# Two fused transformer blocks with 32 experts on one core: expert 1's count, the place of two norm products, and the order of work among the attention heads

## What is computed

```python
def first_block(x, ...):      # conditioned by c
    h = rmsnorm(x, norm1_g) * (1.0 + sc1) + sh1
    xr, yr, q, k, v, ga, gb = split(h @ w_in)
    y_a = rg_lru(causal_dwconv(xr)) * gelu(yr)
    y_b = stick_breaking_attention(norm(q), norm(k), v)
    x = x + gt1 * ((sigmoid(ga) * y_a + sigmoid(gb) * y_b) @ w_out)
    h2 = rmsnorm(x, norm2_g) * (1.0 + sc2) + sh2
    g_ff, v_ff = split(causal_dwconv(h2 @ ffn_up))
    return x + gt2 * ((gelu(g_ff) * v_ff) @ ffn_down)

def second_block(x, ...):
    h = rms_norm(x, g_pre_mix) * (1.0 + sc1) + sh1
    y_mla = mla_attention(...)     # 8 heads
    y_dsa = dsa_attention(...)     # 8 heads, keys picked by an index score
    x = x + gt1 * rms_norm(concat(y_mla, y_dsa) @ w_o, g_post_mix)
    h2 = rms_norm(x, g_pre_ffn) * (1.0 + sc2) + sh2
    # each token goes to its 4 best of 32 experts:
    #   hid = x @ w_mlp1[e] + b1; glu/lin halves; act @ w_mlp2[e] + b2
    return x + gt2 * rms_norm(moe_ffn(h2), g_post_ffn)
```

## Time and profile before

| | |
|---|---|
| median of 3 runs | 1647.08 us (1645.63 to 1647.35) |
| the profiled execution's own time | 1642.82 us |
| its span, first to last instruction | 1641.0 us |
| mean granted TensorE clock | 0.988 of full |
| PE busy | 1570.0 us (96%) |
| VectorE busy | 656.0 us (40%) |
| ScalarE busy | 341.3 us (21%) |
| moved by DMA | 544.95 MB, mean 332 GB/s |
| expert pieces | 384 of 1024 KB |

### The profile page before, as it was taken

The page is one execution under the profiler, slowest core; times in us unless marked ns, Lnnn a source line. Parts: engine busy times, 40 slices in busy tenths (PEclk is TensorE's granted clock), DMA queues, the critical chain, the costliest instruction groups (busy, mean ns, idle before and its releaser), DMA issues. The chain is left out here.

```text
span 1641.0 us, 20583 instructions
## 1 busy us (share of the span) xinstructions
PE 1570.0 (96%) x7248; PEld 882.3 (54%) x7248; DVE 656.0 (40%) x1464; ACT 341.3 (21%) x658; POOL 0.8 (0%) x5
## 2 busy tenths in 40 slices
PE   6999999999999998899999888999999899999997
PEld 4888888888888885433333232333333333333333
DVE  6667862889810663432222222122222312222223
ACT  3126663433200244301010010000010001000001
POOL 0000000000000000000000000000000000000000
PEclk9999999999999999899999998999999899999999
DMA  9937783548963421589999999999999999999995
GB/s 396 420 134 257 256 339 140 188 185 353 411 241 131 154 103 52 213 330 420 420 420 420 419 420 422 416 413 421 420 420 420 420 401 393 422 420 420 420 420 212
DMA packets 77109, 544.95 MB, mean 332 GB/s; under 512 B 8960, under 2 KB 9472, under 8 KB 11424
## 3 DMA queue, kind: packets, MB, share of 16 engines
q1 hardware_dynamic: 75904, 541.79, 81.7%
q10 hardware_dynamic: 1024, 1.18, 0.2%
q0 software_dynamic: 32, 0.00, 0.0%
HBM read 541.89 MB, written 1.05 MB: 331 GB/s over the span
## 5 line engine op out<-in xcount | busy, mean ns | idle before, releaser
L1132 PE MATMUL bank<-ring,scr 128*64 128x512 f32 x1968 | 436.5, 596 | 5.6 <-DMA ring<-in_w_mlp 5.1
L554 PE MATMUL bank<-hT,ring 128*128 128x256 f32 x1472 | 322.5, 380 | 2.0 <-ACT hT L1366 2.0
L554 PEld LDWEIGHTS bank<-hT,ring 128*128 128x128 f32 x1472 | 277.7, 190 | 44.5 <-issue 5.5
L1132 PEld LDWEIGHTS bank<-ring,scr 128*64 128x64 f32 x1968 | 154.7, 138 | 264.9 <-issue 244.1
L1202 PE MATMUL bank<-ring,hT 128*64 128x512 f32 x936 | 216.6, 597 | 1.5 <-DMA ring<-in_w_mlp 1.5
L2622 DVE TENSOR_SCALAR scr<-bank 128x256 f32<-128x256 f32 x64 | 27.0, 422 | 354.5 <-PE bank L1132 354.5
L1202 PEld LDWEIGHTS bank<-ring,hT 128*64 128x64 f32 x936 | 65.5, 136 | 123.9 <-issue 118.0
L2508 DVE TENSOR_TENSOR scr<-bank,mc 128x512 f32<-128x512 f32 x33 | 22.8, 692 | 268.0 <-PE bank L1058 238.4
L1724 ACT ACTIVATE scr<-scr 128x256 f32<-128x256 f32 x64 | 26.8, 418 | 487.0 <-DVE scr L2622 487.0
L1865 DVE SCALAR_TENSOR_TENSOR ring<-ring,con 128x1024 f32<-128x1024 f32 x80 | 94.5, 1219 | 0.0
L751 PE MATMUL bank<-scr,ring 128*128 128x256 f32 x384 | 83.1, 379 | 1.6 <-ACT scr L1541 1.6
(11 more groups left out here) (432 smaller groups left out, 1507.2 us busy)
## 6 DMA issues: line engine op xcount, KB each, us to landing
ring<-in_w_mlp SPq DMA_DIRECT2D x363, 1024.0 KB, 24.2
ring<-in_w_in SPq DMA_DIRECT2D x28, 1024.0 KB, 15.7
ring<-in_up SPq DMA_DIRECT2D x24, 1024.0 KB, 7.0
ring<-in_w_ada SPq DMA_DIRECT2D x24, 1024.0 KB, 6.9
con<-in_w_mlp SPq DMA_DIRECT2D x21, 1024.0 KB, 24.7
ring<-in_ada_w SPq DMA_DIRECT2D x16, 1024.0 KB, 5.4
ring<-in_down SPq DMA_DIRECT2D x12, 1024.0 KB, 15.2
ring<-in_ada SPq DMA_DIRECT2D x8, 1024.0 KB, 19.8
```

Source lines behind the costliest of these rows:

```text
L554: ins = mm(b[:, 256 * j:256 * j + 256], v[:, k * 256 + j * 128:k * 256 + j * 128 + 128], rhs[:, k, :], start=(k == 0), stop=(k == 7))
L1132: ins = mm(HID[0][n][64 * hf:64 * hf + 64, :], K.xe[0][x % 2][:, xo:xo + 64], v[:, o0:o0 + 512], start=(x == 0 and k == 0), stop=(k == 7), ...
```

## The change

Three edits, of order only; no arithmetic is changed. `norm_sum` stands ahead of raw step 4 in both places. Among the heads, step n of PE multiplies head n - 4 (not n - 3), the pairs of scores for heads 10, 12 and 14 are made at the ends of steps 9, 11 and 13 (not at the heads of steps 10, 12 and 14), the last head is multiplied between the halves of the last output step, and both `turn_outputs(1, ...)` come behind it. ScalarE gives expert 1's `n_up`, in a `second_block(1)` that it now runs right after its part of expert 0's activation; VectorE gives the count from expert 2 on.

```diff
--- before.py
+++ after.py
@@ -726,7 +726,7 @@
 
     v = landed(("up", 0))
     for k in range(8):
-        if k == 5:
+        if k == 4:
             norm_sum(1, K.Wt[0])
         ins = raw_step(0, v, B[4:6], k)
     ins.then_inc(S.piece_done, 1)
@@ -968,18 +968,20 @@
             head_turn(n - 3)
         if n < 8:
             head_scores(n)
-        elif n < 16 and n % 2 == 0:
-            two_scores(n)
+        elif n == 8:
+            two_scores(8)
         beside(n)
-        if n == 11:
+        if n == 12:
             e.wait_ge(S.tok, 6)
-        if n >= 3:
-            head_out(n - 3)
+        if n >= 4:
+            head_out(n - 4)
+        if n in (9, 11, 13):
+            two_scores(n + 1)
     e.wait_ge(S.sc_rd, 8)
     out_step(1, 0, 1, 0, 2)
-    e.wait_ge(S.pt, 16)
+    head_out(15)
+    out_step(1, 0, 1, 2, 4).then_inc(S.piece_done, 1)
     turn_outputs(1, 0)
-    out_step(1, 0, 1, 2, 4).then_inc(S.piece_done, 1)
     turn_outputs(1, 1)
 
 
@@ -1708,7 +1710,9 @@
         with e.Else():
             if x:
                 e.wait_ge(S.n_xg, x)
-            else:
+            if x < 2:
+                if x:
+                    e.wait_ge(S.n_up, 8)
                 e.sem_inc(S.n_up, 8)
             e.sem_inc(S.n_xg, 1)
             if x == 0:
@@ -1757,6 +1761,8 @@
                 gather(x + 1)
             if x + 1 < NE:
                 many[x + 1] = crowded(e, K, x + 1)
+            if x == 0:
+                second_block(1)
             if x < NE:
                 e.wait_ge(S.m_at, x + 1)
                 if x >= 2:
@@ -1776,7 +1782,7 @@
                 if x >= 3:
                     e.wait_ge(S.m_pair, 2 * ((x - 1) // 2))
                 act(K.ypair[(x - 1) % 2][0:64, :], K.down_bank(x - 1)[0:64, :], ACT.Copy).then_inc(S.m_ypa, 1)
-            if x + 1 < NE:
+            if 0 < x < NE - 1:
                 second_block(x + 1)
         with e.If(more):
             e.wait_ge(S.m_ypa, NE)
@@ -2598,6 +2604,7 @@
                 e.wait_ge(S.n_selT, x)
                 e.wait_ge(S.n_up, 8 * x)
                 e.wait_ge(S.n_xe, 2 * x)
+            if x >= 2:
                 e.sem_inc(S.n_up, 8)
             e.sem_inc(S.n_xe, 2)
             e.sem_inc(S.n_sel, 1)
```

## The result

The changed kernel took 1626.66 us (median of 4 runs, 1624.13 to 1627.22) beside 1646.36 us for the kernel before (4 runs, 1642.59 to 1647.35): a ratio of 0.9885, 95% interval 0.9869 to 0.9900. Run again later, beside 17 runs of before with a median of 1644.3, it took 1626.84 and the ratio was 0.9895 (0.9881 to 0.9910). So it is 17 to 19 us faster, where 15.0 were forecast. The time of 1632 was missed by 5.3 us: 1626.66 is inside the range of 1624 to 1641, but 1.3 us under the forecast's own stretch of 1628 to 1637. The profiled execution of after took 1627.22 us (span 1625.4) against 1642.82 (span 1641.0) before: 15.6 us.

The account below looks back on a forecast made before the run. TensorE with its waits sets the pace to about 684 us, then the expert-weight stream at about 420 GB/s. Norms 1.7, heads 5.0 and count 8.3 sum to 15.0, from 1647.1 to 1632 us, range 1624 to 1641.

Parts of the forecast that it names:

- norms: Product with ones one raw step sooner at two places; PE's idle behind each falls from 0.99 to 0.12: 1.7 us.
- heads: A whole head between PE's turn and product, scores sooner: stops of 6.2 less new waits of 1.15, net 5.0 us.
- stream: Expert 1's count given earlier by ScalarE lets SP refill the ring and closes the stream's hole: 8.3 us.
- the hole: Stretch from 704 to 716 us where the weight stream ran dry: 8.0 us by share, 8.6 by GB/s, taken as 8.3.
- the four forecast: New PE waits among the heads: head 8's scores 0.45 us, products 7 and 8 0.3 together, output product 0.4.
- cure their cause: Among the heads, sooner scores were to end VectorE's 2.93 us without scores, taken as the cause of PE's stops.
- the room of 4.0 us: Smallest time to spare between a ring place coming free for a new piece and the stream needing it at 707.2.
- the idle of 12.7 us: PE's idle between 860 and 1000 us, where the stream's 8.3 us lead would be used up, with 4.4 left.
- Given back: Rival: the stream, further ahead, just stands longer behind the second crowded expert; only the front gains: 1640 us, chance 0.16.
- Heads only by half: Rival: the heads gain only their lower bound because ScalarE paces: 1635 us, chance 0.08.
- Single pieces each pay in line: Rival: each of the 8 pieces sent singly pays a fixed 2 us in line: 1648 us, chance 0.03.
- Better than the sum: Rival: less idle avoids PE's half clock near 980 to 990, and the hole behind a crowded expert shrinks: 1627 us, chance 0.11.

Follow-up runs that it names:

- the late count: The changed kernel, but ScalarE gives expert 1's count behind its copy in step 0, not ahead of it: 1630.49 us, ratio 0.9911 to the kernel before.
- the delay: The changed kernel with 24 idle products on PE right ahead of expert 0's first piece: 1634.29 us, ratio 0.9952 to the kernel before.

## Why the prediction was right, and where it was off

**The sum against the profiled execution.** 1642.8 - 15.0 = 1627.8; the profiled execution of after took 1627.22. Term by term, in the same pair of profiles:

| us | forecast | measured |
|---|---|---|
| norms | 1.7 | 1.75 |
| heads | 5.0 | 5.23 |
| later start of this execution (0.24), and 0.18 between the heads and the first issue | 0 | -0.42 |
| front in all | 6.7 | 6.55 |
| stream | 8.3 | 9.1 |
| tail | 0 | 0.0 |

Over all profiled executions the stream lasts 936.1 to 938.4 us with the old count (8 of them, mean 937.1) and 926.9 to 929.7 with the new one (5, mean 928.3, the late count left out): 8.8 us. The forecast of 8.3 was the hole alone.

**The norms** went as said, 0.87 and 0.12 forecast, 0.88 and 0.87 won and 0.13 us of idle left, and VectorE's addition wasn't late.

**The heads** were right in size, since the two new waits of 0.5 and 0.2 us are two of the four forecast (0.45 and 0.4) and the 0.3 us of products 7 and 8 didn't come; 5.23 and these 0.77 together are 6.0, near the 6.2 that all stops were put at. The reason given for them was wrong in one step: that the sooner scores "cure their cause". The row of 2.93 us in which VectorE lacked scores was a consequence of PE's stops and no cause: with sooner scores alone PE's waits stay at 4.6 us and VectorE's at 6.1, and with later products alone PE's go and VectorE's fall to 2.5.

**The count**: the whole hole closed, PE was late next, and the room of 4.0 us was confirmed by the late count (6.1 us of delay, 1.8 to 2.2 of hole). The gain held to the end. It was used up where the forecast put it, between 860 and 1000, and from there all moved together; the idle of 8.0 us further back was neither needed nor touched. Of the idle of 12.7 us about 4 were to remain, and 6.35 did. The stretch became 9.05 us shorter; the forecast took all of such a gain from the idle, but 2.7 us of it came from time that counts as busy.

**The rivals.** "Given back" (1640) is out: the stretch behind the second crowded expert is the same at the same work (60 us, PE busy 59.12, 385 and 388 GB/s), so nothing is lost there, and the stream is shorter by the whole hole. "Heads only by half" (1635) is out by the rows of PE. "Single pieces each pay in line" (1648) is out: SP sent the pieces one by one, and from 694 the stream ran at 420 to 428 GB/s; the seven of them issued between 684 and 700 landed after 8.1 us. The Trainium skill, "DMA: Bandwidth & Descriptors", section on the anatomy of one DMA, gives a transfer about 2.0 us fixed beside its bytes; no run here shows that time in line with the data. "Better than the sum" (1627) named the right time, but not by its mechanism: the hole behind the second crowded expert didn't shrink, and PE was still at low clock in the stretch that it named, with 2.5 us of idle (after, columns as before):

```profile
964.00:974.00 10.00, 7.46 (x24) 2.60 (x26) 2.98 (x8) 0.60 (x1) 0.00 (x0) 0.55 1.01 421
```

**The miss of 5.3 us.** It lies almost wholly in the step that carried the sum from the profiled execution to the median. The 4.3 us between them were taken to stay. But the 60 runs of before taken in the whole study have a median of 1644.9, so 2.2 of them were the draw of the first three runs, or of their occasion (the medians of the four later groups of runs are 1644.3 to 1645.8); and after's own profiled execution was the slowest of its four, so the distance didn't stay for it. The rest goes with the clock. Over 56 runs of before the mean granted clock runs from 0.984 (1648.5 us) to 0.991 (1642.3), and time and clock go together (correlation -0.78, and -0.6 to -0.9 inside each of the four groups): 0.20 us for each us of PE at 1.2 GHz. The mean clock of before's runs is 0.9875, that of the eight runs of after 0.991: some 10 us less at the lower level, worth 2.1 us by that slope. At equal clock the two medians are thus 1644.9 - (1626.8 + 2.1) = 16.0 us apart, near the 15.6 of the two profiled executions, both at 0.988. So of the 5.3 us, 2.2 are the draw of three runs, 2.1 go with the clock, and 0.6 to 1.0 are the sum's own. The clock's part rests on that correlation and isn't shown by an experiment: the two that kept PE busy on purpose (ratio 0.9996 among the heads; 1626.6 against 1626.8 ahead of the experts) gained nothing. The profiles point the same way: before's profiled execution had no fall among the heads and none in the last products, and of six others with the old order three and four had one, which puts a typical run above it. Why after's runs spend less time at the lower clock stays open. So does the delay's 7.5 us or more for 5.57 of work; its five runs are back at a mean clock of 0.987.

## What to carry to other kernels

Where a stream of weights sets the end, look for whoever last says that a place is free: if it is an engine that says so for want of another reader, let the one say it whose program comes by earliest, and work out by how much it may be late (here about 4 us). Between a turn, its copy on another engine and the product that reads it, put one whole independent step; making the inputs earlier doesn't help if the product still stands right behind its own copy. Compare two traces at the same work and not at the same time: read at equal times, PE's idle at 1280 to 1330 seems to fall from 8.0 to 3.5 us, and at equal work it doesn't change. And make the sum against one profiled execution, but carry it to the median by the difference of many runs: the median of three was 2.2 us off that of 60, more than the error of the sum itself.

## What the runs showed of the chip

A low clock costs what the place lets through: the router's scores took 1.46 us longer at 1.2 GHz, of which 0.35 or less reached the first issue of the stream, as VectorE set the pace. Where PE is the one waited for, it comes out: up to 1.6 us on a tail of 18.9, in the last group of products (4.11 us instead of 2.48), and some 3.1 us on the front in the profile of the count alone, if the low clock is the whole of it. Where the stream sets the pace, no loss shows: PE had a clock near 0.5 in 964 to 974, and the stream ran at 421 GB/s. Which places are hit differs between executions of one kernel: among the heads of before, in one of three profiles. Filling PE's waits with transposes ahead of the experts shifted the low clock and saved 1.46 us on one group, but no time at the end. And runs of one kernel differ by up to 7 us (1641.5 at a mean clock of 0.990 to 1648.5 at 0.984), so 1 us is hard to tell: with 12 and 17 runs the interval was still 1.4 us to either side.
